# Layer 1's sliding-window attention of the sample tokens: three query heads of one group stacked into one attention unit

## The reference

```
def band_attention(q, kk, vv, sinks, key_valid):
    qg = q.reshape(n, nq, N_KV_HEADS, GROUP, HEAD_DIM)          # 4 groups of 6 heads, width 64
    s = jnp.einsum('nqkgd,njkd->nkgqj', qg, kk) * (HEAD_DIM ** -0.5)
    band = (kj > qi) & (kj <= qi + WINDOW)                      # WINDOW = 128
    s = jnp.where(band & key_valid, s, -jnp.inf)
    m = jnp.maximum(jnp.max(s, axis=-1, keepdims=True), sink)   # one sink score per head
    e = jnp.exp(s - m)
    p = e / (jnp.sum(e, axis=-1, keepdims=True) + jnp.exp(sink - m))
    o = jnp.einsum('nkgqj,njkd->nqkgd', p, vv)
```

## Time and profile before

| what | us |
|---|---|
| median of 9 runs | 3882.76 (3870.25 to 4247.71) |
| the profiled execution | 3873.72 |
| span of its slowest core (core 4) | 3872.2 |
| spans of its 8 cores | 3855.4 to 3872.2, granted clock 0.896 to 0.899 |
| sample units of layer 1, first to last reduce | 2491.38 to 2585.82 |
| output projection of layer 1 starts | 2648.51 |

### The profile page before, as it was taken

One profiled execution on the slowest core, in us unless ns is written; L12 is line 12 of the kernel. 1 busy time (PEld: TensorE's weight loads), 2 busy tenths in 40 slices (PEclk: granted clock), 3 DMA queues, 4 the chain that ended last, 5 costly groups with the idle time before them and its releaser, 6 DMA issues.

```text
span 3872.2 us, 61298 instructions; the slowest of 8 cores (3855.4 to 3872.2 us)
## 1 busy us (share of the span) xinstructions
PE 3420.6 (88%) x21228; PEld 1778.9 (46%) x21228; DVE 1467.2 (38%) x3563; ACT 703.7 (18%) x2085; POOL 452.5 (12%) x538
## 2 busy tenths in 40 slices
PE   5578885597999998799998899988799999999995
PEld 4433334353555554355553345554344444444442
DVE  2222323224333333133334467873433333333334
ACT  1111222202000000000001356672200000000003
POOL 0012223200111111111100000000111111111100
PEclk7779897597999999899998899757899999999996
DMA  9679999943565656466555662603547666666632
GB/s 154 134 77 127 105 139 117 126 62 37 64 68 66 66 66 66 46 68 67 63 71 75 81 88 42 79 2 50 55 55 77 75 68 77 68 74 73 70 44 90
DMA packets 716034, 293.63 MB, mean 76 GB/s; under 512 B 523844, under 2 KB 690180, under 8 KB 712982
## 3 DMA queue, kind: packets, MB, share of 16 engines
q0 software_dynamic: 708896, 263.22, 61.8%
q1 hardware_dynamic: 6840, 26.50, 2.0%
HBM read 541.74 MB, written 12.12 MB: 143 GB/s over the span
## 4 chain that ended last, share of the span: by engine, by line
PE 78%; DMA 10%; DVE 5%; ACT 3%; issue 3%; POOL 1%; ACTq 0%; SPq 0%; DVEq 0%; POOLq 0%
PE bank L317 76%; DMA sb_slot<-conv_w_in 6%; PE bank L320 2%; ACT sb_rb L323 2%; DVE sb_ra L332 2%; DMA sb_ra<-xe 2%; DMA sb_rb<-cmk 1%; DVE sb_rb L420 1%; ACT sb_ptr L323 1%; DVE sb_rb L332 1%; DVE sb_st L475 1%; DMA sb_ra<-mem 1%; DVE sb_ra L347 0%; POOL sb_slot L341 0%; DMA sb_rc<-cwv 0%
## 5 line engine op out<-in xcount | busy, mean ns | idle before, releaser
L317 PE MATMUL bank<-sb_ra,sb_slot 128*128 128x512 bf16 (+2 forms) x9984 | 1607.6, 321 | 18.3 <-DVE sb_ra L332 18.2
L317 PE MATMUL bank<-sb_rb,sb_slot 128*128 128x512 bf16 (+4 forms) x7136 | 1243.7, 332 | 104.2 <-DMA sb_slot<-conv_w_in 81.0
L317 PEld LDWEIGHTS bank<-sb_ra,sb_slot 128*128 128x128 bf16 x9984 | 805.0, 97 | 818.7 <-issue 30.0
L317 PEld LDWEIGHTS bank<-sb_rb,sb_slot 128*128 128x128 bf16 x7136 | 619.7, 100 | 681.1 <-issue 152.9
L326 DVE TENSOR_TENSOR sb_rx<-sb_rx,bank 128x512 f32<-128x512 f32 (+2 forms) x1152 | 616.2, 544 | 353.3 <-PE bank L317 318.0
L326 DVE TENSOR_TENSOR sb_rb<-sb_rc,bank 128x512 bf16<-128x512 f32 (+2 forms) x264 | 143.6, 544 | 1205.2 <-PE bank L317 1205.2
L323 ACT ACTIVATE sb_rc<-bank 128x512 f32<-128x512 f32 (+7 forms) x363 | 169.4, 468 | 2175.7 <-PE bank L317 2035.5
L341 POOL DMA_DIRECT2D sb_slot<-w_gate x88 | 100.6, 1144 | 1179.6 <-PE bank L317 1179.6
L317 PE MATMUL bank<-sb_rb,sb_onesb 128*128 128x512 bf16 (+4 forms) x272 | 108.5, 414 | 77.8 <-ACT sb_rb L323 72.4
L323 ACT ACTIVATE sb_rb<-sb_rx 128x512 bf16<-128x512 f32 (+3 forms) x240 | 114.8, 513 | 328.4 <-PE bank L317 288.4
L323 ACT ACTIVATE sb_er<-bank,sb_st 128x257 bf16<-128x257 f32 (+3 forms) x388 | 172.0, 443 | 3.6 <-DVE sb_st L484 1.7
(11 more groups left out here) (74 smaller groups left out, 1425.4 us busy)
## 6 DMA issues: line engine op xcount, KB each, us to landing
sb_slot<-w_gate POOLq DMA_DIRECT2D x88, 512.0 KB, 8.6
sb_slot<-w_up POOLq DMA_DIRECT2D x88, 512.0 KB, 10.5
sb_slot<-w_down POOLq DMA_DIRECT2D x44, 1024.0 KB, 9.0
sb_slot<-conv_w_in POOLq DMA_DIRECT2D x72, 512.0 KB, 16.1
sb_slot<-attn_w_in POOLq DMA_DIRECT2D x30, 1024.0 KB, 9.3
sb_slot<-conv_w_in POOLq DMA_DIRECT2D x24, 1024.0 KB, 19.0
sb_ra<-xe SPq DMA_DIRECT2D x9, 1024.0 KB
sb_slot<-w_mem_kv POOLq DMA_DIRECT2D x8, 1024.0 KB, 22.0
```

The costliest lines, as they stand in the source:

```text
L317: P.op("pe", lambda e: e.matmul(out, lhsT=lhsT, rhs=rhs, start=start, stop=stop), r=r, w=w)
```

## The change

The three even heads of a group become one unit, and the three odd heads another: 24 queries on 24 partitions, head by head, against the one key head that they share. This makes 32 sample units out of 96. [...] The last stage writes its 24 columns back to three chunks by one cast. The mask gets a third table (the 8 rows of the band, three times), and the sinks a second form, one column for each of the 8 pairs of group and half, 24 rows; this makes one more DMA and three more DVE operations at the start.

```
-    mask_d = din("mask", [128, 512])
+    mask_d = din("mask", [128, 768])
+    sinks24_d = din("sinks24", [128, 8])
...
+    Qs = View(RB, 0, (16, 24), BF16)
...
-        DMA("sp", [(mstg.ap, mask_d.rearrange("p (a b) -> p a b", a=2))], [], mstg.r(), "mstg")
+        DMA("sp", [(mstg.ap, mask_d.rearrange("p (a b) -> p a b", a=3))], [], mstg.r(), "mstg")
...
+        DMA("sp", [(s24f[:, 0, :], sinks24_d[:, :])], [], ["s24f"], "s24f")
+        cp("dve", snk24[:, 0, :], s24f[:, 0, :], ["s24f"], ["snk24"])
+        TT("dve", s24f[:, 1, :], s24f[:, 0, :], snk24[:, 0, :], ALU.subtract, ["s24f", "snk24"], ["s24f"])
+        cp("dve", snk24[:, 1, :], s24f[:, 1, :], ["s24f"], ["snk24"])
...
         def s7():
-            cp("dve", out_ap, d["bt3"][p0:p1, 128:128 + nq], [d["br3"]], out_res)
+            src = d["bt3"][p0:p1, 128:128 + nq]
+            cp("dve", out_ap, src if out_src is None else out_src(src), [d["br3"]], out_res)
...
         for s in range(4):
             c0 = C_SAMP + 8 * s
             for g in range(4):
-                for hh in (0, 2, 4, 1, 3, 5):
-                    h = 6 * g + hh
-                    c, par = h // 2, h % 2
+                for par in range(2):
...
-                    units.append(attn_unit(8, mixT.ap[p0:p1, c, c0:c0 + 8], mixT.r(c, (c0, c0 + 8)), sKT.ap[p0:p1, s, g, :], sKT.r(s, g), 136,
-                                           maskb[:8, 0, 0:136], h, vch, mixT.ap[p0:p1, c, c0:c0 + 8], mixT.r(c, (c0, c0 + 8)), p0, p1))
+                    qa = mixT.ap[p0:p1, 3 * g:3 * g + 3, c0:c0 + 8]
+                    qr = mixT.r((3 * g, 3 * g + 3), (c0, c0 + 8))
+                    units.append(attn_unit(24, Qs.ap[p0:p1, 4 * s + g, :], Qs.r(4 * s + g), sKT.ap[p0:p1, s, g, :], sKT.r(s, g), 136,
+                                           maskb[:24, 2, 0:136], 2 * g + par, vch,
+                                           qa, qr, p0, p1, snk_t=snk24, out_src=lambda a: a.rearrange("p (j q) -> p j q", j=3)))
...
         flush_feed()
+        def gatherq(_):
+            for s4 in range(4):
+                for g in range(4):
+                    c0 = C_SAMP + 8 * s4
+                    cp("pool", Qs.ap[:, 4 * s4 + g, :].rearrange("p (j q) -> p j q", j=3), mixT.ap[:, 3 * g:3 * g + 3, c0:c0 + 8],
+                       mixT.r((3 * g, 3 * g + 3), (c0, c0 + 8)), Qs.r(4 * s4 + g))
+        item(gatherq)
         for c in steps[168:]:
             item(c)
```

More of the change, by code:

```diff
@@ L239, in build @@
     yT = View(RA, 0, (16, 128), F32)
-    mstg = View(RA, 34816, (2, 256), F32)
+    mstg = View(RA, 34816, (3, 256), F32)
     ostg = [View(RA, 8192 + 8192 * i, (D,), F32) for i in range(2)]
@@ L280, in build @@
     onesb = P.sb("onesb", [128, 128], BF16)
-    maskb = P.sb("maskb", [128, 2, 256], BF16)
+    maskb = P.sb("maskb", [128, 3, 256], BF16)
     onesf = P.sb("onesf", [1, 128], F32)
@@ L284, in build @@
     snk = P.sb("snk", [128, 2, 24], BF16)
+    snk24 = P.sb("snk24", [128, 2, 8], BF16)
+    s24f = P.sb("s24f", [128, 2, 8], F32)
     snkf = P.sb("snkf", [128, 24], F32)
@@ L448, in build, with attn_unit @@
     NST = 8
[L450 removed]
+    def attn_unit(nq, q_ap, q_res, kt_ap, kt_res, nk, mask_ap, sink_ap, vch, out_ap, out_res, p0, p1, xsets=False, pre=None, snk_t=None, out_src=None):
         d = {}
@@ L465, in s0 @@
                 MM(bt[:nq, :nk], identb[:nq, :nq], mask_ap, False, True, ["identb", "maskb"], [br])
-                MM(bt[:nq, nk:ne], identb[:nq, :nq], snk[:nq, 0, sink_ap:sink_ap + 1], True, False, ["identb", "snk"], [br])
-                MM(bt[:nq, nk:ne], identb[:nq, :nq], snk[:nq, 1, sink_ap:sink_ap + 1], False, True, ["identb", "snk"], [br])
+                sk = snk if snk_t is None else snk_t
+                MM(bt[:nq, nk:ne], identb[:nq, :nq], sk[:nq, 0, sink_ap:sink_ap + 1], True, False, ["identb", "snk", "snk24"], [br])
+                MM(bt[:nq, nk:ne], identb[:nq, :nq], sk[:nq, 1, sink_ap:sink_ap + 1], False, True, ["identb", "snk", "snk24"], [br])
             else:
@@ L1001, in make_in_maps @@
     m_first = np.where(band & (kj >= 128), 0.0, NEG).astype(np.float32)
+    m_s24 = np.full((128, 256), NEG, np.float32)
+    m_s24[0:24] = np.tile(m_std[0:8], (3, 1))
+    sk = np.asarray(inp["attn_sinks"], np.float32)[0]
+    s24 = np.zeros((128, 8), np.float32)
+    for g_ in range(4):
+        for par_ in range(2):
+            for j_ in range(3):
+                s24[8 * j_:8 * j_ + 8, 2 * g_ + par_] = sk[6 * g_ + 2 * j_ + par_]
     shared = {k: np.ascontiguousarray(np.asarray(inp[k], np.float32)) for k in ("w_mem_kv", "w_gate", "w_up", "w_down")}
+    shared["sinks24"] = s24
     shared["conv_w_in"] = np.ascontiguousarray(np.asarray(inp["conv_w_in"], np.float32)[0])
@@ L1026, in make_in_maps @@
         m["cmv"] = np.ascontiguousarray(np.asarray(inp["cache_mem_v"], np.float32)[:, 4 * c:4 * c + 4].reshape(2, 4, 256, 512))
-        m["mask"] = np.ascontiguousarray(np.stack([m_std, m_first if hf == 0 else m_std], axis=1).reshape(128, 512))
+        m["mask"] = np.ascontiguousarray(np.stack([m_std, m_first if hf == 0 else m_std, m_s24], axis=1).reshape(128, 768))
         maps.append(m)
```

## The result

The five runs of the changed kernel that enter the ratio took 3819.31, 3819.65, 3825.41, 3835.44 and 3837.41 us; the middle one is 3825.41, where 3825 was forecast. The ratio to the kernel before is **0.9866**, with a 95% interval from 0.9849 to 0.9884. The profiled execution took 3819.31 us with a span of 3817.8 on its slowest core, core 7: 54.4 less than the profiled execution before; the sum had said 53.7.

What follows compares the result with a forecast made beforehand. The sample stage was held bound by a pipeline of short instructions, each step costing their starts. Terms -63.6 + 1.9 + 7.0 + 1.0 = -53.7 us took 3873.72 to 3820.0; plus 5 offset, 3825, range 3808 to 3842.

Steps and rivals of the forecast that it cites:

- the sum: Whole kernel: the predicted terms added up, -53.7 us, taking the profiled execution from 3873.72 to 3820.0 us.
- Fewer units: Layer 1 sample attention: 96 units become 32, so 64 fewer pipeline steps of 0.994 us each, -63.6 us.
- Wider units: Sample stage: 16 more columns in copies, matmuls and cast add 0.06 us to each of 32 steps, +1.9 us.
- The rival of 128-query steps: Sample stage: a 24-query unit costs as much as a 128-query one, 1.25 us a step, 3831 us; chance 0.11.
- Order of the halves: Sample stage: alternating even and odd units leaves the mean step unchanged, as the cost goes with the odd half; no term.
- The gather: End of layer 1's projection: POOL's query copies hold up a prompt unit's cast through a shared 512-byte piece, +7.0 us.
- The rival in which the stall never reaches the end: After the projection: the wait at the gather is made up for, 3818 us without the 7.0; chance 0.08.
- The start: Kernel start: one more DMA and a mask larger by 128 KB delay the memory rows PE waits for, +1.0 us.
- the 17 us named as a sign of being wrong: Kernel start: a first memory transpose later than 17 us would count against the forecast.
- The clock: Output projection: rival that PE's clock stays at 1.2 GHz, costing 119 us more, 3944 us; chance 0.04.
- The offset: Whole kernel: the median run stands above the profiled execution, +5 us, giving 3825.

Runs made afterwards that it cites:

- the run with eight: Changed kernel with 8 instead of 24 queries in each of its 32 sample units; 30.88 us from first to last reduce, against 31.46.
- The sorted order: Changed kernel with all 16 even sample units first, then all 16 odd ones, instead of alternating; 31.46 us from first to last reduce.
- gather alone: Kernel before plus the 16 POOL copies into Qs, never read; scaling to output projection 197.15 us against 189.64; one execution, 3910.95 us.
- fine pieces: Changed kernel with dependency tracking of region ra in 4-byte instead of 512-byte pieces; 3802.7 us, ratio to the kernel before 0.9804.
- the two experiments on the kernel before: Kernel before with only the POOL gather copies added (197.15 us from scaling to output projection), and kernel before with only 4-byte tracking pieces (3862.95 us).
- finer pieces alone: Kernel before with region ra tracked in 4-byte instead of 512-byte pieces, without the change; 3862.95 us, ratio 0.9959.

## Why the prediction was right, step by step

- *Fewer units*, -63.6: right. The reduces lost 63.0, and the sum for them (-63.6 + 1.9) was -61.7. That the length of a step hardly depends on how many queries it holds is shown by the run with eight: 0.996 against 1.015 with 24. It does depend on the instructions: with one more score matmul, one more cast and 64 rows it is 1.22.
- *Wider units*, +1.9: the mechanism was right, the size was not; it is 0.6. I let PE's 66 ns reach the path nearly whole, where the step took up 19 of it. The rival of 128-query steps (1.25) falls.
- *Order of the halves*, 0: right within half a microsecond. The sorted order takes the same 31.46, with 10 odd casts in place of 13 in the window; at 0.15 for each that is some 0.4 us in favour of alternating, which I estimate and no run separates.
- *The gather*, +7.0: right in place, cause and size. The cast waited for POOL and came 7.4 later behind its scaling; gather alone cost 7.5, and fine pieces took the wait away. Most of the 0.4 that were missing are the copies' spacing, 0.34 in place of 0.32 over 14 gaps. The rival in which the stall never reaches the end falls with the gather alone, as far as the output projection.
- *The start*, +1.0: at the first memory transpose the median core is 1.2 later (15.18 to 16.35; in the two experiments on the kernel before, without the new constants, 15.14 and 15.21). Two of the eight cores come later than the 17 us named as a sign of being wrong (17.20 and 17.40). Whether the 1.2 lasts to the end stays open: the arrival at the last scaling scatters by more than ten times as much.
- *The clock* rival falls: the granted clock is at 1.00 within 4.57 us of the output projection.
- *The offset*, +5, from a profiled execution to the middle run: it is 6.1 here (3819.31 to 3825.41), with five runs that spread over 18 us. Before, it is 5.0 to the middle of the 26 runs that enter the ratio (3873.72 to 3878.70); the 9.0 of the prediction goes to the median of nine.

The errors were small and partly cancelled: the width came 1.3 under its term, the stall 0.4 over, and the rest of the stretch 0.8 under. So the stretch shrank by 56.4, where the sum had said 54.7. On the two profiled cores it was 56.1, and 0.8 more went behind it, but core 7 came to its last scaling 2.5 later than core 4 had before; that makes the 54.4, near the 53.7 by luck, since this arrival scatters by 18 us and more. That the middle run lies 0.4 from the forecast is luck too.

## What to carry to other kernels

In a software pipeline of short instructions, count the steps and read the length of one from the trace; stacking independent small problems into a step is worth nearly the number of steps that it removes. When an edit adds an operation, look up who else touches the same piece of memory in the kernel's dependency tracking, however small the operation: 16 copies that were needed 30 us later stopped an unrelated cast for 7 us. Then ask the same of the whole program: finer pieces alone took some 12 us off this kernel, in a place where no one was looking.

## What had not been expected of the hardware

POOL copies of 128x24 that each wait for the one before start 0.34 us apart, though one takes only 0.20; two other copies had led to 0.32. The odd half's cast makes a step 0.15 us longer (1.07 against 0.92), and not by its own duration (0.19 against 0.16) alone: it starts 0.11 later behind its reduce, and the reduce after it 0.10 later behind the scaling, while the reciprocal between them comes 0.06 sooner. And a pipeline whose steps are all alike can still swing between 0.78 and 1.08 us a step; the longer steps hold a wait of DVE for ACT, but why it comes in every second step was not settled.
